# Small inputs packed side by side and replicated by the host, in a two-layer transformer block on one core

## The reference

```python
for layer in range(DEPTH):
    h = h + hybrid_mixer(rms_norm(h, attn_norm[layer]), positions, layer, w_in[layer], ...)
    hn = rms_norm(h, ffn_norm[layer])
    if layer % 2 == 0:
        h = h + swiglu(hn, dense_w_gate[j], dense_w_up[j], dense_w_down[j])
    else:
        h = h + moe_ffn(hn, moe_router[j], moe_w_gate[j], moe_w_up[j], moe_w_down[j])
return rms_norm(h, final_norm)
```

## Time and profile before

| what | value |
|---|---|
| median of three runs | 1678.57 us (1674.35, 1679.5, 1678.57) |
| the profiled execution | 1676.76 us, its span 1675.0 us |
| granted TensorE clock, mean | 0.947 of full |
| PE busy | 1596.9 us (95%) |
| DVE busy | 1271.3 us (76%) |
| ACT busy | 1034.2 us (62%) |
| POOL busy | 61.1 us (4%) |
| bytes moved | 431.10 MB, 427.11 MB of them on SP's queue, 3.25 MB on ACT's |

### The profile page before, as it was taken

One profiled execution on the slowest core, in us unless ns is written; L12 is line 12 of the kernel. 1 busy time (PEld: TensorE's weight loads), 2 busy tenths in 40 slices (PEclk: granted clock), 3 DMA queues, 4 the chain that ended last, 5 costly groups with the idle time before them and its releaser, 6 DMA issues.

```text
span 1675.0 us, 20863 instructions
## 1 busy us (share of the span) xinstructions
PE 1596.9 (95%) x7246; PEld 1296.6 (77%) x7246; DVE 1271.3 (76%) x1562; ACT 1034.2 (62%) x1320; POOL 61.1 (4%) x128
## 2 busy tenths in 40 slices
PE   6979999999898998999999999999999999999996
PEld 5857788888686677888888888888888888888885
DVE  4676555555547646989989989989989989989995
ACT  4334354444334335778778778778778778778774
POOL 1400000000032000000000000000000000000000
PEclk9965999999898578999999999999999999999999
DMA  8311265455251024999999999999989999999992
GB/s 270 132 51 51 101 219 199 166 188 179 82 181 65 1 102 165 369 335 358 352 338 357 349 336 363 351 326 367 350 326 366 350 327 365 351 328 359 358 362 104
DMA packets 184456, 431.10 MB, mean 257 GB/s; under 512 B 6352, under 2 KB 13008, under 8 KB 184400
## 3 DMA queue, kind: packets, MB, share of 16 engines
q1 hardware_dynamic: 180272, 427.11, 70.2%
q10 hardware_dynamic: 4128, 3.25, 0.6%
HBM read 429.30 MB, written 1.05 MB: 257 GB/s over the span
## 4 chain that ended last, share of the span: by engine, by line
PE 89%; DVE 5%; ACT 3%; issue 2%; DMA 1%; DVEq 0%; POOL 0%; SPq 0%
PE pair L765 47%; PE work L765 32%; PE work L741 3%; PE work L984 2%; PE pair L741 2%; PE pair L823 1%; PE work L752 1%; PE work L893 1%; ACT w_hi L1085 1%; ACT arena L1216 1%; DMA ring<-in_w_in 1%; DVE nmax L1475 1%; DVE w_lo L1388 0%; DVE arena L1566 0%; PE work L998 0%
## 5 line engine op out<-in xcount | busy, mean ns | idle before, releaser
L1388 DVE TENSOR_TENSOR w_lo<-ring,w_hi 128x1024 fp32r<-128x1024 f32 (+2 forms) x812 | 968.7, 1214 | 254.4 <-ACT w_hi L1085 248.6
L1085 ACT ACTIVATE w_hi<-ring 128x1024 fp32r<-128x1024 f32 (+2 forms) x812 | 849.4, 1054 | 350.0 <-PE pair L765 186.6
L765 PE MATMUL pair<-w_hi,hnT_hi 128*128 128x512 f32 x1120 | 448.5, 400 | 5.1 <-DVE hnT_lo L1396 3.0
L765 PE MATMUL pair<-w_lo,hnT_hi 128*128 128x512 f32 x1120 | 442.6, 395 | 0.0
L765 PE MATMUL pair<-w_hi,hnT_lo 128*128 128x512 f32 x1120 | 442.5, 395 | 0.0
L765 PEld LDWEIGHTS pair<-w_hi,hnT_hi 128*128 128x128 f32 x1120 | 210.5, 188 | 53.5 <-DVE hnT_lo L1396 3.6
L765 PEld LDWEIGHTS pair<-w_hi,hnT_lo 128*128 128x128 f32 x1120 | 210.4, 188 | 50.9
L765 PEld LDWEIGHTS pair<-w_lo,hnT_hi 128*128 128x128 f32 x1120 | 210.6, 188 | 47.6
L765 PE MATMUL work<-w_hi,hidT_hi 128*128 128x512 f32 x552 | 219.7, 398 | 2.6 <-DVE hidT_lo L1634 1.4
L765 PE MATMUL work<-w_lo,hidT_hi 128*128 128x512 f32 x552 | 218.3, 395 | 0.0
L765 PE MATMUL work<-w_hi,hidT_lo 128*128 128x512 f32 x552 | 218.3, 395 | 0.0
(11 more groups left out here) (177 smaller groups left out, 1111.1 us busy)
## 6 DMA issues: line engine op xcount, KB each, us to landing
ring<-in_moe_w_gate SPq DMA_DIRECT2D x56, 2048.0 KB, 8.1
ring<-in_moe_w_up SPq DMA_DIRECT2D x56, 2048.0 KB, 8.5
ring<-in_moe_w_down SPq DMA_DIRECT2D x56, 2048.0 KB, 7.9
ring<-in_dense_w_gate SPq DMA_DIRECT2D x7, 2048.0 KB, 7.8
ring<-in_dense_w_up SPq DMA_DIRECT2D x7, 2048.0 KB, 7.7
ring<-in_dense_w_down SPq DMA_DIRECT2D x7, 2048.0 KB, 7.6
ring<-in_w_in SPq DMA_DIRECT2D x4, 2048.0 KB, 8.1
ring<-in_w_out SPq DMA_DIRECT2D x4, 2048.0 KB, 8.0
```

The costliest lines, as they stand in the source:

```text
L765: mm = pe.matmul(b, lhs[x_part][k + kk], w[w_part][:, kk, :], start=(first and kk == 0 and i == 0), stop=(last and kk == 1 and i == 2))
L1085: return act.activation(o, i, ACT.Copy)
L1388: dve.tensor_tensor(lo, raw, hi.bitcast(F32), ALU.subtract).then_inc(lo_done, 1)
```

## The change

The host builds four packed arrays. `setup` holds, for each of the 128 partitions, all lambda vectors (256 numbers), the 16 frequencies and the partition's two positions: 274 words, 1096 bytes. `norm_gains` holds the five rows of norm gains, each repeated 128 times. `layer_gains` holds for each layer the 448 numbers of its three small gain rows, repeated 128 times: 1792 bytes a partition. `router` is laid out as the kernel's tile is, 64 words a partition. At the start ACT issues three transfers in the order gain, `setup`, `layer_gains`. `load_layer_gains` issues one transfer where it issued three. SP no longer waits for `loaded_small` before `PI`. The frequencies move into the arena beside the lambdas, and `lamp` moves from row 1 to row 7 of the same region, since `setup` now runs over into row 1. The matrix weights are passed and read as before.

```diff
-        freq = sb("freq", [P, NF])
-        cgain = sb("cgain", [P, CQ + CKV])
-        sgain = sb("sgain", [P, 2 * DB])
+        layer_gains = sb("layer_gains", [P, CQ + CKV + 2 * DB])
+        cgain, sgain = layer_gains[:, 0:CQ + CKV], layer_gains[:, CQ + CKV:]
...
+        n_lam = DEPTH * 4 * DB
+        setup = qcT_all[:, 0:n_lam + NF + T]
+        lamv = setup[:, 0:n_lam].rearrange("p (l v d) -> p l v d", l=DEPTH, v=4)
+        freq = setup[:, n_lam:n_lam + NF]
+        pos_i = setup[:, n_lam + NF:].bitcast(I32)
+        lamp = qcT[:, 7, 0:DEPTH * 2 * DB].rearrange("p (l v d) -> p l v d", l=DEPTH, v=2)
...
-                    if (layer, c) == (0, "PI"):
-                        sp.wait_ge(loaded_small, 16 * 6)
...
-            def load_gain(v):
-                act.dma_start(gain[:, :], row(v, D)).then_inc(loaded_gain, 16)
+            def load_gain(which):
+                act.dma_start(gain[:, :], a["norm_gains"][NORMS.index(which)]).then_inc(loaded_gain, 16)
 
             def load_layer_gains(layer):
-                act.dma_start(cgain[:, 0:CQ], row(a["mla_q_norm"][layer], CQ)).then_inc(loaded_cgain, 16)
-                act.dma_start(cgain[:, CQ:], row(a["mla_kv_norm"][layer], CKV)).then_inc(loaded_cgain, 16)
-                act.dma_start(sgain[:, :], row(a["diff_subln"][layer], 2 * DB)).then_inc(loaded_cgain, 16)
+                act.dma_start(layer_gains[:, :], a["layer_gains"][layer]).then_inc(loaded_cgain, 16)
...
-            with nc.allow_non_contiguous_dma(reason="the positions, one to a partition"):
-                act.dma_start(pos_i, positions.rearrange("a (t p) -> p (a t)", p=P)).then_inc(loaded_small, 16)
-            load_gain(a["attn_norm"][0])
-            act.dma_start(freq[:, :], row(a["rope_freq"], NF)).then_inc(loaded_small, 16)
-            for i, name in enumerate(("q1", "k1", "q2", "k2")):
-                v = a[f"diff_lambda_{name}"]
-                act.dma_start(lamv[:, :, i, :], v.unsqueeze(0).to_broadcast([P, DEPTH, DB])).then_inc(loaded_small, 16)
+            load_gain(("attn", 0))
+            act.dma_start(setup, a["setup"]).then_inc(loaded_small, 16)
             load_layer_gains(0)
...
-                            act.dma_start(router, a["moe_router"][0].rearrange("(k p) e -> p k e", p=P)) \
+                            act.dma_start(router, a["router"]) \
                                 .then_inc(loaded_router, 16)
...
+        "setup": np.concatenate([everywhere(lambdas), everywhere(freq), places], axis=1),
+        "norm_gains": np.stack([everywhere(v) for v in (
+            f["attn_norm"][0], f["ffn_norm"][0], f["attn_norm"][1], f["ffn_norm"][1], f["final_norm"])]),
+        "layer_gains": np.stack([everywhere(np.concatenate([f[n][layer] for n in (
+            "mla_q_norm", "mla_kv_norm", "diff_subln")])) for layer in range(depth)]),
+        "router": router.reshape(-1, P, router.shape[1]).transpose(1, 0, 2).reshape(P, -1),
```

More of the change, by code:

```diff
@@ L82, in hybrid_block @@
 def hybrid_block(nc, a, out):
-    x, positions = a["x"], a["positions"]
+    x = a["x"]
     S, D = x.shape[1], x.shape[2]
@@ L243, in hybrid_block @@
         pt = qiT_or_pt.rearrange("p (b k s) -> p b k s", b=2, k=4)
-        qcT = carve(HC * S).rearrange("p (k s) -> p k s", k=HC)
+        qcT_all = carve(HC * S)
+        qcT = qcT_all.rearrange("p (k s) -> p k s", k=HC)
         kcT = carve(HC * S).rearrange("p (k s) -> p k s", k=HC)
@@ L247, in hybrid_block @@
         score = carve(T * S).rearrange("p (t s) -> p t s", t=T)
-        lamv = qcT[:, 0, :].rearrange("p (l v d) -> p l v d", l=DEPTH, v=4)
-        lamp = qcT[:, 1, 0:DEPTH * 2 * DB].rearrange("p (l v d) -> p l v d", l=DEPTH, v=2)
+        n_lam = DEPTH * 4 * DB
[4 more added lines that the diff above has]
+        lamp = qcT[:, 7, 0:DEPTH * 2 * DB].rearrange("p (l v d) -> p l v d", l=DEPTH, v=2)
         lams = qcT[:, 2, 0:2 * DEPTH].rearrange("p (l v) -> p l v", l=DEPTH)
         lame = qcT[:, 2, 64:64 + 2 * DEPTH].rearrange("p (l v) -> p l v", l=DEPTH)
-        pos_i = qcT[:, 3, 0:T].bitcast(I32)
         pos_f = qcT[:, 3, 64:64 + T]
@@ L262, in hybrid_block @@
         hnT = carve(KT * S).rearrange("p (k s) -> p k s", k=KT)
-        router = carve(KT * E).rearrange("p (k e) -> p k e", k=KT)
+        router = carve(KT * E)
         before = carve(P)
@@ L1061, in _ @@
                     emptied(pe, (1, "XF", t, i))
-                product(b, E, [hnT[:, k, tile(t)] for k in range(KT)], [router[:, k, :] for k in range(KT)]) \
+                product(b, E, [hnT[:, k, tile(t)] for k in range(KT)], [router[:, k * E:(k + 1) * E] for k in range(KT)]) \
                     .then_inc(job_done, 1)
@@ L1085, in copy @@
                 return act.activation(o, i, ACT.Copy)
-            def row(v, n):
-                return v.rearrange("(a n) -> a n", a=1).to_broadcast([P, n])
-            def load_gain(v):
-                act.dma_start(gain[:, :], row(v, D)).then_inc(loaded_gain, 16)
+            def load_gain(which):
+                act.dma_start(gain[:, :], a["norm_gains"][NORMS.index(which)]).then_inc(loaded_gain, 16)
             def load_layer_gains(layer):
-                act.dma_start(cgain[:, 0:CQ], row(a["mla_q_norm"][layer], CQ)).then_inc(loaded_cgain, 16)
-                act.dma_start(cgain[:, CQ:], row(a["mla_kv_norm"][layer], CKV)).then_inc(loaded_cgain, 16)
-                act.dma_start(sgain[:, :], row(a["diff_subln"][layer], 2 * DB)).then_inc(loaded_cgain, 16)
+                act.dma_start(layer_gains[:, :], a["layer_gains"][layer]).then_inc(loaded_cgain, 16)
             def squares(which, t):
@@ L1168, in attention @@
                             act.wait_ge(normed, norm_count(("attn", layer), t))
-                            load_gain(a["ffn_norm"][layer])
+                            load_gain(("ffn", layer))
                     elif name == "PI":
@@ L1268, in dense @@
                         act.wait_ge(normed, norm_count(("ffn", 0), 1))
-                        load_gain(a["attn_norm"][1])
+                        load_gain(("attn", 1))
                         act.wait_ge(d_normed, T)
@@ L1337, in _ @@
             act.wait_ge(normed, norm_count(("ffn", 1), 1))
-            load_gain(a["final_norm"])
+            load_gain(("final", 1))
             turn_evac((1, "XF", 1, 0), ("XF", 1, 0))
@@ L1402, in angles @@
             def angles():
-                dve.wait_ge(loaded_small, 16 * 6)
+                dve.wait_ge(loaded_small, 16)
                 link(dve.tensor_copy(pos_f, pos_i))
                 for t in range(T):
-                    last = dve.tensor_scalar(ang[:, t, :], freq[:, :], pos_f[:, t:t + 1], None, ALU.mult)
+                    last = dve.tensor_scalar(ang[:, t, :], freq, pos_f[:, t:t + 1], None, ALU.mult)
                 link(last)
@@ L1514, in attention @@
                         dve.wait_ge(c_rms, layer * T + t + 1)
-                        dve.wait_ge(loaded_cgain, 48 * (layer + 1))
+                        dve.wait_ge(loaded_cgain, 16 * (layer + 1))
                         for i, (c0, c1) in enumerate(((0, CQ), (CQ, CQ + CKV))):
@@ L1521, in attention @@
                         if t == 0:
-                            link(dve.tensor_scalar(sgain[:, :], sgain[:, :], 1.0 - LAM_INIT[layer], None, ALU.mult))
+                            link(dve.tensor_scalar(sgain, sgain, 1.0 - LAM_INIT[layer], None, ALU.mult))
                     elif name == "CT":
@@ L1606, in attention @@
                                                ALU.mult))
-                        dve.tensor_tensor(o, o, bc(sgain[:, :], [P, HB, 2 * DB]), ALU.mult).then_inc(d_normed, 1)
+                        dve.tensor_tensor(o, o, bc(sgain, [P, HB, 2 * DB]), ALU.mult).then_inc(d_normed, 1)
                     elif name == "WO":
@@ L1832, in _ @@
                 norm(("final", 1), t).then_inc(out_ready, 1)
[L1835 to L1838, removed]
+_WEIGHTS = ("w_in", "w_uq", "w_ukv", "w_out", "dense_w_gate", "dense_w_up", "dense_w_down",
+            "moe_w_gate", "moe_w_up", "moe_w_down")
 def kernel(**inputs):
@@ L1846, with everywhere @@
     nc = bacc.Bacc("TRN2", target_bir_lowering=False, num_devices=1)
-    arrays = {n: np.ascontiguousarray(inputs[n]) for n in _INS}
-    arrays["rope_freq"] = (THETA ** (-np.arange(16) / 16.0)).astype(np.float32)
+    f = {n: np.asarray(v) for n, v in inputs.items()}
+    depth = f["attn_norm"].shape[0]
+    def everywhere(v):
+        return np.broadcast_to(v, (P,) + v.shape)
+    lambdas = np.stack([f[f"diff_lambda_{n}"] for n in ("q1", "k1", "q2", "k2")], axis=1).reshape(-1)
+    freq = (THETA ** (-np.arange(16) / 16.0)).astype(np.float32)
+    places = np.ascontiguousarray(f["positions"].reshape(-1, P).T).astype(np.int32).view(np.float32)
+    router = f["moe_router"][0]
+    arrays = {
+        "x": f["x"],
+        "setup": np.concatenate([everywhere(lambdas), everywhere(freq), places], axis=1),
[4 more added lines that the diff above has]
```

(4 more changed lines are left out.)

## The result

| kernel | median, us | lowest to highest | executions |
|---|---|---|---|
| before | 1678.50 | 1674.35 to 1679.69 | 20 |
| changed | 1681.56 | 1678.51 to 1683.94 | 20 |

The ratio is 1.0021, with a 95% interval of 1.0015 to 1.0028. The changed kernel is 0.2% slower: 3.1 us, where 2.3 us less had been forecast. The profiled execution took 1683.9 us (span 1682.1), so it lies 2.4 us over its median, as that of the kernel before lay 1.7 us under its own. Comparing the two spans alone (7.1 us) overstates the loss.

The account below looks back on a forecast made before the run. PE's matmul chain was taken to bound the kernel, with transfers deciding only the opening. `PC` landing sooner gave 2.3 us, other terms nothing: 1675.0 us from the mean of 1677.3, range 1669 to 1681.

Parts of the forecast that it names:

- The landing and the first product: Opening: `PC` lands at 13.5 instead of 15.82, so the first product moves from 17.94 to 15.6, by 2.3 us.
- the rate between 9 and 13: DMA in the opening: 267 GB/s before; staying thin puts `PC` at 14.5, some 390 GB/s puts it at 12.9.
- the norm: Opening, first tile of `x`: starts near 8.6 instead of 11.60, held by the landing of the gains.
- the branch of `x`: Opening, squares to `hnT_lo`: moves by 3.0 us, worth nothing by itself, nearly decides if `PC` lands at 12.9.
- Layer 1 and the experts as before, earlier by the same 2.3 us: After the opening: the later program keeps its times and only starts 2.3 us sooner.
- the slower side: Whole kernel: chance 0.07 of a slower result, 0.04 from sharing with `PI` and `PK`, 0.03 from a longer slow clock.
- Whatever moves 17.94 earlier moves the whole rest earlier: From the first product on: PE's chain follows its start, so the 2.3 us gained there reach the end.
- The prediction's last sign: If the difference at 60 us is not that at the end, the clock decided and not the transfers.
- The landing doesn't move: Rival, opening: same bytes, so `PC` lands as before; 1676.8 to 1677.3 us, no change; chance 0.13.
- `PI` and `PK` take `PC`'s place: Rival, opening: engines share the three transfers, `PC` lands about 5 us later; 1682 us, 0.3% slower; chance 0.07.
- A slow stretch of the clock goes as well: Rival: all moves and the lower clock soon after 30 is avoided; 1669 to 1672 us; chance 0.13.
- The costs taken as nothing: SP's wait before `PI`, `angles()` waiting for `setup`, and layer 1's small gain issues: each put at nothing.

Follow-up runs that it names:

- the kernel with the pad: The changed kernel with an unused 64-byte buffer where `freq` stood, so everything behind it lies at the old addresses: 1676.18 us, ratio 0.9988 to the kernel before.
- with the transposes: The changed kernel with 60 transposes of the identity on PE before its first real work: 1679.97 us, ratio 1.0018 to the kernel before.

## Why the prediction was wrong

**The landing and the first product came as summed.** `PC` landed at 12.9 (13.5 forecast, 12.9 the near bound) and the first product came at 15.45 (15.6), 2.5 us sooner. With the split weights at the old address the changed kernel has ratios of 0.9988, 0.9983 and (with SP's wait) 0.9979: 2.0 to 3.5 us faster, with the forecast of 2.3 among them.

**Two terms inside it were off and cancelled.** The rate between 9 and 13 rose more than I allowed, to 405 GB/s. And the norm began at 9.46 and not near 8.6. The gains were there at 6.6, but the first tile of `x` landed at 6.4 and not at 5.0, and the list puts `N1` of both tiles ahead of `N2` of the first, so DVE first handled the second tile's mean, for whose squares ACT waited until 8.18 for `x`. ACT went straight from `hnT_hi` to `w_hi` at 13.36, after `PC` had landed: the branch of `x` has become the later one by 0.4 us, as the prediction said it nearly would.

**The step that failed is the one on the rest of the program.** "Layer 1 and the experts as before, earlier by the same 2.3 us" put the matmuls' own time at no change. Weights are indeed there before they are wanted, and where the host's arrays lie doesn't matter there. But the change also moved things on the chip: `freq` left the list of buffers, and every buffer declared behind it moved down by 64 bytes, `w_hi` and `w_lo` among them, the moving operands of every large matmul. I read that line of the diff and costed only the transfer that went with it. That term was worth 5.7 us in the changed kernel (1681.89 to 1676.18 on one chip) and 6.4 in the kernel before (0.38%). In the profiled pair it is 0.4% in the dense net and the experts, 4.8 us, and in the 2.3 us between them about 0.9 by the same 0.4%; the rest, some 1.4 us by this estimate, is a longer stretch at the lower clock in layer 1. No rival in the prediction had this mechanism, so the slower side had 0.07 where it needed more, and the range ended 0.6 us short.

**A smaller step failed beside it.** "Whatever moves 17.94 earlier moves the whole rest earlier" does not hold in each execution. With a slow start of PE the products of `PC` themselves take about 2 us more: the kernel with the pad had its first product 2.5 us sooner than the kernel before and reached the 1001st matmul at the same 256.2. The kernel with 64 bytes ahead of `w_hi` started fast and kept 2.8 us. That the forecast of 2.3 fits the medians supposes that slow starts are about as common in either kernel. The prediction's last sign, a difference at 60 us that is not that at the end, did show, but it would have blamed the clock alone, and most of the loss was the address.

**The rivals.** "The landing doesn't move" is refuted: 2.9 us sooner with 0.06 MB more in ACT's queue. The prediction had tied this rival to the Trainium skill's section "Issuing engines are not separate DMA queues", which speaks only of the time that issuing takes and doesn't say that the bytes alone set a landing. What the Trainium skill's page "DMA: Bandwidth & Descriptors", table "Specifications", says of transfers under 512 bytes agrees with the rates in the windows, but the replicated source changed along with the packets and no run separates the two. "`PI` and `PK` take `PC`'s place" is refuted by the changed kernel itself and by the kernel before without the wait. "A slow stretch of the clock goes as well" did not happen near 29 in the profiled pair (a granted share of 0.58 after 0.57 from 30 to 34). It did in the kernel with the 64 bytes and SP's wait, where the granted clock stays at 1.00 from 30 to 34 and the 96 products take 18.64 us in place of 20.20. So the clock went both ways: it helped some executions of the kernels at the old address, and in layer 1 it hurt those at the new one.

**The costs taken as nothing** (SP's wait, layer 1's issues, `angles()`) were nothing. The small gains of layer 1 are issued in 0.45 us, and ACT's wait behind them is 1.75 us after 1.74, and `angles()` began at 19.23, right behind the second tile's `hnT_lo`.

## What to carry to other kernels

A change that adds, drops or resizes a buffer moves all those declared behind it: list the addresses of the operands of the hot loop before and after, and hold them fixed with a pad before you judge the change. Count instructions in a fixed window when a duration differs only in its last digit. And when a kernel is bound by matmuls, try its moving operand at a multiple of 128 bytes; here that was worth 29 us, some twelve times the 2.3 us that the repacking of the inputs was to bring.

## What the runs showed of the hardware

The speed of matmuls in fp32r (the 4-byte float type of the split operands) whose moving operand has 512 columns depended on the byte at which that operand begins. By the chain's 24 products: 234.2 ns each at a rest of 32 to 128, 233.3 at 64 and 96, 226.7 at 0. The stationary operands (`hnT_hi`, `hnT_lo`, and `hidT_hi` in the arena) began at multiples of 128 in all kernels, so what their address does was not tried; nor was a rest that is not a multiple of 32. Why 32 is worse than 96 stays open, and that the reading of the moving operand is the cause is argued from the unchanged times of its two writers, not measured by itself.

The address also went with the clock. From the 1822nd to the 2755th matmul the four profiles at a rest of 32 (the changed kernel twice, with the transposes, and the kernel before moved by 64 bytes) took 233.7 to 237.0 us, with a granted share of 0.73 to 0.76 from 450 to 620. The seven at 64 and 96 took 231.5 to 231.7, with 0.78 or 0.79. By what way slightly longer matmuls bring a longer stretch at the lower level is not shown.

PE began the program at the lower clock level: 16 transposes took 3.6 us at the start of both kernels and 1.76 us behind the added ones. When it reached the upper level differed by execution: the products were at 0.19 us from 18.2 on in the kernel before, from 19.7 in the changed one and from 21.9 in the kernel before at the address with rest 0, and from 15.5 in the changed one with 64 bytes ahead of `w_hi`. The column of the granted clock stood at 1.00 all the while. The Trainium skill's page "TensorE: Matmul & The Clock Gate", Part 1, says that the number of slow matmuls at a kernel's start varies from run to run; these profiles agree, with 12 slow products of `PC` in the changed kernel and none in the one with 64 bytes ahead of `w_hi`.
